# Two moves of VectorE and GpSimd work around the second and third output projections of a three-layer kernel

## The chip, the cores and the metric

The kernel runs on one core of one Trainium2 chip. The metric is the device time of one execution in microseconds (us). Before the change it was 1709.45 us, the median of three runs (1708.28 to 1711.23).

The core's engines each follow their own instruction list: TensorE (PE, matrix products), VectorE (DVE), ScalarE (ACT), GpSimd (POOL) and SyncE (SP), which here does nothing but issue loads and stores. They meet only at semaphores. An instruction whose semaphore has not been reached holds up everything behind it in the list of its engine, and on SP that means every later load.

## The reference, cut to what matters

One sequence of 256 tokens of width 1024 passes three layers. The first is a hybrid attention with a mixture of 16384 small experts. The other two are the same in form:

```python
mod = silu(c) @ ada_w[i] + ada_b[i]           # six vectors of 1024: shifts, scales, gates
h = modulate(rms_norm(x, g0), sh1, sc1)
y = mixer(h)                                  # i = 0: nsa; i = 1: sliding window ("swa"); each ends with o @ w_out
x = x + (1 + g1) * rms_norm(y, g1n)
h = modulate(rms_norm(x, g2n), sh2, sc2)
y = relu(h @ w_up)**2 @ w_down                # 1024 -> 4096 -> 1024
x = x + (1 + g2) * rms_norm(y, g3n)
```

The product `silu(c) @ ada_w` has one row, so it is not made by TensorE: VectorE multiplies a block of the transposed weights (128 output columns as partitions, 1024 inputs) by the broadcast row and sums. One such block is a "modulation block" or "piece" here. The last four vectors that are computed take 32 of them.

## The kernel before, in words

**Weights.** All weights except the modulation's come as a stream of 512 KB chunks (128 x 1024 floats) into a ring of eight slots. Chunk `c` may be loaded into its slot once chunk `c - 8` has been used (`chunk_used`). A product is made in three passes of reduced-precision parts: the high part of a chunk is rounded off by ACT (`high`, into one of four buffers, after chunk `c - 4` has been used), the low part is the difference of chunk and high part and is written over the chunk, by DVE or by POOL (`low`). A list, `BY_DVE`, says which chunks' low parts are DVE's; the rest of the split chunks are POOL's. TensorE waits for the low part of a chunk before it uses it. The first two chunks of some products are "pairs", whose high parts have buffers of their own (`pair_high`, `pair_low`).

**Stages.** The code of each engine is written out in the order of the stages. The ones that matter are: attention of the second layer (`att2`), its output projection (`out2`, eight chunks), end of the branch (`branch_end(0)`: y's squares by ACT, gating, residual sum and norm by DVE, transposes by TensorE, the high and low parts of the new activations), the MLP (`mlp2`, 64 chunks), `branch_end(1)`, the third layer's input projection with rotary embedding (`swa`, 10 chunks), attention (`att3`), output projection (`out3`, eight chunks), `branch_end(2)` and `mlp3`.

**The MLP.** Chunks of `w_up` and `w_down` alternate: in `mlp2`, up block `j` is chunk `2j - 2` for `j` from 2 to 29, and down block `j - 2` is chunk `2j - 1`; up 30 and 31 are chunks 58 and 59, and the last four down blocks are chunks 60 to 63. DVE's part is `hidden(name)`. Step `j` (0 to 31) squares ACT's relu of block `j` and splits it (`one(j)`), makes the low parts of one chunk (steps 0, 1, 30, 31) or of two, chunks `2j + 2` and `2j + 3` (steps 2 to 29), and, in `mlp2` only, uses one modulation piece (`ada(j)`): piece `j + 4`, in steps 0 to 27. Pieces 0 to 3 are used before that, in front of `branch_end(0)`.

**SP's order.** Modulation pieces have two buffers. `load_ada_mlp(i)` waits until piece `i - 2` has been used (`ada_used`), issues the load, and only then does SP come to the next chunk of the ring. In the MLP its loop is, for `k` from 0: load chunk `8 + 2k`, load piece `k + 6`, load chunk `9 + 2k`. Ahead of the loop SP issues pieces 0 and 1, chunks 0 to 3, pieces 2 and 3, chunks 4 to 7, pieces 4 and 5.

**Output projections.** In `out2` the low parts of the first four chunks are DVE's (two of them in the last two steps of `att2`, two after it) and POOL makes the other four. In `out3` all eight are POOL's.

Of the kernel before, what the change touches and what calls it, by code (L numbers as in the profile page):

```python
# [40 lines left out]
DB = D // P  # L41
# [10 lines left out]
HIGHS = 4  # L52
# [20 lines left out]
for _name, _n in STREAM:  # L73
# [12 lines left out]

BY_DVE = [FIRST_CHUNK[name] + i for name, first, n in [("qk1", 0, 2), ("wq", 2, 16), ("v", HIGHS, NKEYS), ("nsa", 2, 20), ("out2", 0, HIGHS),
                                                    ("mlp2", 2, 64), ("swa", 2, 10), ("mlp3", 2, 64)] for i in range(first, n)]
BY_POOL = [c for c in SPLIT if c not in BY_DVE]  # L90
NTH_BY_DVE = {c: i for i, c in enumerate(BY_DVE)}
NTH_BY_POOL = {c: i for i, c in enumerate(BY_POOL)}
# [140 lines left out]
ADA_LAYER3 = [A_NF + D, A_NF + 2 * D]  # L233
ADA_ORDER = [*range(6), 12, 13, 8, 9, 10, 6, 7, 11, 15, 16, 14, 17]
AT = {v: i for i, v in enumerate(ADA_ORDER)}
# [9 lines left out]
def two_blocks(nc, a):  # L245
    ctx = ExitStack()
    with ctx:
# [176 lines left out]
        def plan(kinds, unit0, step0, order=lambda s: 0):  # L424
            steps, unit = [], unit0
            for g in range(4):
                for t in range(TT):
                    ks = kinds(g)
                    for n, kind in enumerate(ks):
                        steps.append(dict(kind=kind, unit=unit, t=t, g=g, first=n == 0, last=n == len(ks) - 1))  # L430
                    unit += 1
            steps.sort(key=order)
            return [dict(s, n=step0 + i) for i, s in enumerate(steps)]
        att1 = plan(lambda g: ["moba" if g < 2 else "dsa"], 0, 0)
        att2 = plan(lambda g: ["sel", "win", "cmp"], 8, 8, lambda s: (s["g"], s["g"] == 0 and s["last"]))
        att3 = plan(lambda g: ["swa"], 16, 32)
# [5 lines left out]
        chunk = FIRST_CHUNK  # L442
# [186 lines left out]
        @block.gpsimd  # L629
        def _(pool):  # L630
            def low(c, more=0):
                pool.wait_ge(S["high_ready"], more + (NTH_SPLIT[c] + 1))
                pool.tensor_tensor(WL[:, c % SLOTS, :], ring[:, c % SLOTS, :], WH[:, c % HIGHS, :], ALU.subtract)\  # L633
                    .then_inc(S["low_by_pool"], 1)

            def lows(lo, hi):
                rounds = (hi - lo) // SLOTS
                if rounds:
                    with pool.Fori(0, rounds) as r:
                        for s in range(SLOTS):  # L640
                            low(lo + s, r * SLOTS)
                for c in range(lo + rounds * SLOTS, hi):
                    low(c)

            def split_done(n):
                pool.wait_ge(S["ht_low"], DB * (n + 1))
            pool.wait_ge(S["low_by_dve"], 2)
            lows(2, chunk["wq"])
            split_done(1)
            lows(chunk["u"], chunk["v"])  # L650
            lows(chunk["v"], chunk["v"] + HIGHS)
            pool.wait_ge(S["chunk_used"], chunk["nsa"] + 8)
            pool.memset(A(A_VCC, D + 4 * 2 * N_CMP), 0.0).then_inc(S["cmp_zeroed"], 1)  # L653
            lows(chunk["out2"] + HIGHS, chunk["mlp2"])
            lows(chunk["out3"], chunk["mlp3"])

        @block.tensor
# [995 lines left out]
        def _(dve):  # L1654
# [20 lines left out]
            def ada_piece(i, landed, slots, v, landed_more=0):  # L1675

                dve.wait_ge(S[f"{landed}{i % 2}"], landed_more + 16 * (i // 2 + 1))
                ada_block(A(slots[i % 2], D), v, i % DB)
# [34 lines left out]
            def low(c, more=0):  # L1713
                dve.wait_ge(S["high_ready"], more + (NTH_SPLIT[c] + 1))
                dve.tensor_tensor(WL[:, c % SLOTS, :], ring[:, c % SLOTS, :], WH[:, c % HIGHS, :], ALU.subtract)\  # L1715
                    .then_inc(S["low_by_dve"], 1)
# [81 lines left out]
            def attention(steps, beside=lambda i: None):  # L1798

                maxima(steps[0])  # L1800
                for i, s in enumerate(steps):
                    if i > 2 and steps[i - 3]["last"]:
                        y_low(steps[i - 3])
                    if i + 1 < len(steps):
                        maxima(steps[i + 1])
                    scale_probs(s)
                    beside(i)
                for s in steps[-3:]:
                    if s["last"]:
                        y_low(s)  # L1810
# [356 lines left out]
            for kv in range(2):  # L2167
                dve.wait_ge(S[f"z_loaded{kv}"], 64)
                for half_window in range(2):
                    first = 16 * half_window  # L2170
# [44 lines left out]
                    low(first + i)  # L2215

            def ada_mlp(i, r=None):
                ada_piece(i, "ada_mlp", ADA_LAYER3, 15 if i < DB and r is None else bass.ds(AT[15] + i // DB, 1) if r is None else
                          bass.ds(r + (AT[15] + i // DB), 1), 0 if r is None else r * (16 * DB // 2))

            def hidden(name):
                c0, o0, base = chunk["mlp" + name], OUTS["up" + name], 32 * (int(name) - 2)

                def ada(j, r=None):
                    if name == "2":
                        ada_mlp(j + 4, r)

                def one(j, more=0):
                    s = j % 2
                    dve.wait_ge(S["out_taken"], more + (o0 + j + 1))  # L2230
                    done = more + (base + j + 1)
                    dve.tensor_tensor(RELU[:, s, :], RELU[:, s, :], RELU[:, s, :], ALU.mult).then_inc(S["relu_squared"], 1)
                    dve.wait_ge(S["relu_squared"], done)
                    dve.tensor_copy(HIDH[:, j % HIDS, :], RELU[:, s, :]).then_inc(S["hidden_high"], 1)
                    dve.wait_ge(S["hidden_high"], done)
                    dve.tensor_tensor(HIDL[:, j % HIDS, :], RELU[:, s, :], HIDH[:, j % HIDS, :], ALU.subtract)\
                        .then_inc(S["hidden_ready"], 1)

                for j in range(2):
                    one(j)  # L2240
                    low(c0 + j + 4)
                    ada(j)
                for j in range(2, 4):
                    one(j)
                    low(c0 + 2 * j + 2)
                    low(c0 + 2 * j + 3)
                    ada(j)
                with dve.Fori(0, 3) as r:
                    for j in range(4, 12):
                        one(j, r * 8)  # L2250
                        low(c0 + 2 * j + 2, r * 16)
                        low(c0 + 2 * j + 3, r * 16)
                        ada(j, r)
                for j in (28, 29):
                    one(j)
                    low(c0 + 2 * j + 2)
                    low(c0 + 2 * j + 3)
                for j in (30, 31):
                    one(j)
                    low(c0 + 32 + j)  # L2260
# [1 line left out]
            low(chunk["out2"] + 2)  # L2262
            low(chunk["out2"] + 3)
            for i in range(2):
                ada_mlp(i)
            for i in range(2, 4):
                ada_mlp(i)
            for i in range(2):
                pair_low(chunk["mlp2"] + i)
# [12 lines left out]
                    low(chunk["swa"] + m + 2)  # L2282
                roped(ROPES3, ROPE2, lambda i: KD[:, i, :] if i < 2 else Q2[:, i - 2, :], m)
            dve.wait_ge(S["sink_loaded"], 16)
            attention(att3)
            for i in range(2):
                pair_low(chunk["mlp3"] + i)
            branch_end(2, chunk["mlp3"])
# [71 lines left out]
```

## Time and profile before

| what | value |
|---|---|
| median of three runs | 1709.45 us |
| the profiled execution, device time | 1708.28 us |
| its span in the profile | 1706.5 us |
| PE busy | 1638.2 us, 96% |
| VectorE busy | 1222.7 us, 72% |
| ScalarE busy | 908.9 us, 53% |
| GpSimd busy | 449.7 us, 26% |
| read from memory | 341 MB, 200 GB/s over the span |
| mean granted TensorE clock | 0.986 of full |

The span is the time from the first to the last instruction in the trace; 1.8 us lie around it. A busy share is a mean over stages that have different limits, so the question at each place is which wait ends last there.

### The profile page before, as it was taken

Reading aid. Unit: us, or ns where it says so; the run is one execution under the profiler, and the core shown is the slowest. Engines: PE = TensorE matmul, PEld = TensorE weight load, DVE = VectorE, ACT = ScalarE, POOL = GpSimd, SP = SyncE. Lnnn points to the kernel's source line nnn. Section 1 sums busy time; section 2 is a strip of 40 time slices with the busy share of each in tenths; the row PEclk is TensorE's granted clock in tenths of the full one; section 3 lists DMA queues with packets and bytes.
Section 4 is the critical chain, followed back from the end, with each engine's and each line's share of the span. In section 5 each row is a group of like instructions: output and inputs, shape, how many; then the busy total and the mean of one; then the engine's idle time right before and its main releaser. Section 6 shows DMA issues by size and latency. Waiting matters only on the chain.

```text
span 1706.5 us, 31170 instructions
## 1 busy us (share of the span) xinstructions
PE 1638.2 (96%) x10735; PEld 1442.5 (85%) x10740; DVE 1222.7 (72%) x2382; ACT 908.9 (53%) x1747; POOL 449.7 (26%) x181
## 2 busy tenths in 40 slices
PE   6988999999999998999999999998899999799998
PEld 3975899999999998788888878965699998489997
DVE  5369869599618993888877867747598877766665
ACT  4445554455469994454554565358544445664443
POOL 0970138989875556000000000000200000120000
PEclk9999999999999999999999999989999999999999
DMA  9877775555553334988888765540477766145553
GB/s 341 308 189 237 268 221 185 181 180 181 184 172 112 111 111 155 319 293 294 287 288 286 239 227 155 163 160 1 148 274 281 285 218 147 52 148 185 186 189 105
DMA packets 105527, 344.26 MB, mean 202 GB/s; under 512 B 18483, under 2 KB 22339, under 8 KB 105444
## 3 DMA queue, kind: packets, MB, share of 16 engines
q1 hardware_dynamic: 101092, 339.19, 59.3%
q10 hardware_dynamic: 4352, 4.02, 0.8%
q8 instruction: 46, 0.75, 0.2%
q14 instruction: 37, 0.30, 0.1%
HBM read 341.02 MB, written 1.10 MB: 200 GB/s over the span
## 4 chain that ended last, share of the span: by engine, by line
PE 80%; issue 5%; POOL 5%; DVE 4%; ACT 3%; DMA 2%; ACTq 1%; SPq 0%; POOLq 0%; DVEq 0%
PE banks L675 23%; PE banks L676 23%; PE banks L677 23%; POOL weights_low L633 5%; PE banks L981 3%; DMA ada_ring<-in_ada 1%; PE banks L840 1%; PE banks L807 1%; PE banks L856 1%; DMA arena<-in_ada 1%; ACT arena L1298 1%; PE banks L708 1%; PE banks L712 1%; PE banks L709 1%; DVE arena L1788 0%
## 5 line engine op out<-in xcount | busy, mean ns | idle before, releaser
L1244 ACT ACTIVATE weights_high<-ring 128x1024 fp32r<-128x1024 f32 x470 | 494.9, 1053 | 333.5 <-PE banks L677 321.4
L633 POOL TENSOR_TENSOR weights_low<-ring,weights_high 128x1024 fp32r<-128x1024 f32 x176 | 448.4, 2562 | 666.5 <-ACT weights_high L1244 666.0
L675 PE MATMUL banks<-ht_high,weights_high 128*128 128x256 f32 x1936 | 556.8, 288 | 4.1 <-DVE ht_low L1743 4.1
L676 PE MATMUL banks<-ht_low,weights_high 128*128 128x256 f32 x1936 | 547.9, 283 | 0.0
L677 PE MATMUL banks<-ht_high,weights_low 128*128 128x256 f32 x1936 | 547.8, 283 | 0.0
L1715 DVE TENSOR_TENSOR weights_low<-ring,weights_high 128x1024 fp32r<-128x1024 f32 x294 | 358.3, 1223 | 87.7 <-ACT weights_high L1244 86.9
L675 PEld LDWEIGHTS banks<-ht_high,weights_high 128*128 128x128 f32 x1936 | 371.2, 192 | 7.4 <-issue 4.1
L676 PEld LDWEIGHTS banks<-ht_low,weights_high 128*128 128x128 f32 x1936 | 371.5, 192 | 2.6
L677 PEld LDWEIGHTS banks<-ht_high,weights_low 128*128 128x128 f32 x1936 | 371.1, 192 | 0.0
L675 PE MATMUL banks<-weights_high,ga_parts 128*128 128x512 f32 x504 | 197.5, 392 | 9.3 <-DVE ga_parts L2047 9.2
L676 PE MATMUL banks<-weights_low,ga_parts 128*128 128x512 f32 x504 | 196.7, 390 | 0.0
L677 PE MATMUL banks<-weights_high,ga_parts 128*128 128x512 f32 x504 | 196.6, 390 | 0.0
L1500 ACT ACTIVATE ga_parts<-arena 128x256 fp32r (+1 forms) x126 | 52.5, 417 | 173.4 <-PE banks L677 173.4
L1666 DVE SCALAR_TENSOR_TENSOR arena<-arena,cs 128x1024 f32<-128x1024 f32 x80 | 106.5, 1342 | 50.0 <-DMA arena<-in_ada 45.0
L675 PEld LDWEIGHTS banks<-weights_high,ga_parts 128*128 128x128 f32 x504 | 95.0, 188 | 31.2 <-POOL weights_low L633 4.4
L677 PEld LDWEIGHTS banks<-weights_high,ga_parts 128*128 128x128 f32 x504 | 95.0, 189 | 19.9
L676 PEld LDWEIGHTS banks<-weights_low,ga_parts 128*128 128x128 f32 x504 | 95.1, 189 | 19.6
L653 POOL MEMSET arena<- 128x1144 f32 x1 | 1.1, 1052 | 390.3 <-PE banks L677 390.3
L675 PE MATMUL banks<-weights_high,hidden_high 128*128 128x512 f32 x256 | 100.3, 392 | 0.0
L676 PE MATMUL banks<-weights_low,hidden_high 128*128 128x512 f32 x256 | 100.3, 392 | 0.0
L677 PE MATMUL banks<-weights_high,hidden_low 128*128 128x512 f32 x256 | 99.6, 389 | 0.0
L2004 DVE TENSOR_TENSOR arena<-arena,banks 128x512 f32<-128x512 f32 (+1 forms) x64 | 44.0, 688 | 61.1 <-PE banks L981 55.6
(274 smaller groups left out, 2288.6 us busy)
## 6 DMA issues: line engine op xcount, KB each, us to landing
ring<-in_stream SPq DMA_DIRECT2D x490, 512.0 KB, 3.5
arena<-in_ada SPq DMA_DIRECT2D x88, 512.0 KB, 5.3
ada_ring<-in_ada SPq DMA_DIRECT2D x56, 512.0 KB, 4.3
arena<-gate_store SPq DMA_DIRECT2D x5, 512.0 KB, 5.9
arena<-bias_rows ACTq DMA_DIRECT2D x1, 2048.0 KB, 20.3
X<-in_x SPq DMA_DIRECT2D x1, 1024.0 KB, 6.1
out<-X SPq DMA_DIRECT2D x4, 256.0 KB, 2.1
arena<-arena ACTq DMA_DIRECT2D x8, 127.5 KB, 4.7
```

The costliest lines, as they stand in the source:

```text
L633: pool.tensor_tensor(WL[:, c % SLOTS, :], ring[:, c % SLOTS, :], WH[:, c % HIGHS, :], ALU.subtract)\
L675: pe.matmul(out, wh, xh, start=start, stop=False, **kw)
L676: pe.matmul(out, wh, xl, start=False, stop=False, **kw)
L677: return pe.matmul(out, wl, xh, start=False, stop=stop, **kw)
L708: pe.matmul(outs[n], wh[:, k * P:(k + 1) * P], HTH[:, k, :], start=i == 0 and n == 0, stop=False, skip_group_check=True)
L709: pe.matmul(outs[n], wl[:, k * P:(k + 1) * P], HTH[:, k, :], start=False, stop=False, skip_group_check=True)
L981: m = pe.matmul(banks[:, 2 + s, q * P:(q + 1) * P], onehot[:, s, 0, q, :], onehot[:, s, 1, q, :], start=True, stop=True)
L1244: act.activation(WH[:, c % HIGHS, :], ring[:, c % SLOTS, :], ACT.Copy).then_inc(S["high_ready"], 1)
L1500: act.activation(gated(j)[:, 0, :], src, ACT.Copy).then_inc(S["ga_high_ready"], 1)
L1666: dve.scalar_tensor_tensor(out=w, in0=w, scalar=1.0, in1=cs[:], op0=ALU.mult, op1=ALU.mult, accum_out=column)\
L1715: dve.tensor_tensor(WL[:, c % SLOTS, :], ring[:, c % SLOTS, :], WH[:, c % HIGHS, :], ALU.subtract)\
L2004: dve.tensor_tensor(g, g, banks[:, 2 + group % ONEHOTS, :].rearrange("p (t j) -> p j t", t=4), ALU.mult)\
```

## The change

The two pieces 2 and 3 are no longer used before `branch_end(0)`. `ada(j)` now uses piece `j + 2`, so that all pieces from 2 on lie two steps later in `hidden("2")`, and steps 28 and 29 get one each. SP's code is not touched. In `out3` the low parts of the first four chunks go from POOL to DVE: two in the last two steps of `att3`, two behind it.

```diff
 BY_DVE = [... ("nsa", 2, 20), ("out2", 0, HIGHS),
-                                                    ("mlp2", 2, 64), ("swa", 2, 10), ("mlp3", 2, 64)] for i in range(first, n)]
+                                                    ("mlp2", 2, 64), ("swa", 2, 10), ("out3", 0, HIGHS), ("mlp3", 2, 64)] for i in range(first, n)]
...
             lows(chunk["out2"] + HIGHS, chunk["mlp2"])
-            lows(chunk["out3"], chunk["mlp3"])
+            lows(chunk["out3"] + HIGHS, chunk["mlp3"])
...
                 def ada(j, r=None):
                     if name == "2":
-                        ada_mlp(j + 4, r)
+                        ada_mlp(j + 2, r)
...
                 for j in (28, 29):
                     one(j)
                     low(c0 + 2 * j + 2)
                     low(c0 + 2 * j + 3)
+                    ada(j)
...
             for i in range(2):
-                ada_mlp(i)
-            for i in range(2, 4):
                 ada_mlp(i)
...
-            attention(att3)
+
+            def beside_att3(step):
+                if step >= len(att3) - 2:
+                    low(chunk["out3"] + step - (len(att3) - 2))
+            attention(att3, beside_att3)
+            for i in range(2, HIGHS):
+                low(chunk["out3"] + i)
```

VectorE's list at the end of `out2`. L1666 is a modulation piece, L1720 the low part of a pair, L2196 the gating of y; `ada_mlp0` and `ada_mlp1` are the landings in the two buffers:

```order
 L1666 SCALAR_TENSOR_TENSOR arena,mod<-arena,cs 128x1024 [waits ada_mlp0]
 L1666 SCALAR_TENSOR_TENSOR arena,mod<-arena,cs 128x1024 [waits ada_mlp1]
-L1666 SCALAR_TENSOR_TENSOR arena,mod<-arena,cs 128x1024 [waits ada_mlp0]
-L1666 SCALAR_TENSOR_TENSOR arena,mod<-arena,cs 128x1024 [waits ada_mlp1]
 L1720 TENSOR_TENSOR weights_low<-ring,pair_high 128x1024 [waits pair_high] x2
 L2196 TENSOR_TENSOR arena<-banks,arena 128x512 [waits y_sums,gate_rows_ready]
```

Two pieces, and the wait for their landing, have left the place between `out2` and the gating of its result.

SyncE's list at the start of `mlp2`, which is the same before and after (L477 loads a modulation piece, L469 a chunk of the ring):

```order
L477 DMA arena<-in_ada 128x1024 [waits ada_used] x2
L604 UNCONDITIONAL_BRANCH
L604 ISA
L469 ISA [waits chunk_used]
L469 DMA ring<-in_stream 128x1024
L474 ISA
L477 ISA [waits ada_used]
L477 DMA arena<-in_ada 128x1024
L467 REGISTER_ALU
L469 ISA [waits chunk_used]
L469 DMA ring<-in_stream 128x1024
```

Nothing moved here: each load of a piece still stands ahead of a load of a chunk, and waits for a piece that VectorE now uses two steps later.

VectorE's list at the end of `att3`. L1788 scales probabilities, L1795 is a low part of the attention's result, L1715 the low part of a chunk:

```order
 L1788 TENSOR_SCALAR arena<-arena,rsum 128x256 [waits dve_link]
 L1788 TENSOR_SCALAR arena<-arena,rsum 128x256 x3
+L1715 TENSOR_TENSOR weights_low<-ring,weights_high 128x1024 [waits high_ready]
 L1795 TENSOR_TENSOR ht_low<-banks,ht_high 128x2x128 [waits y_high_ready] x3
+L1715 TENSOR_TENSOR weights_low<-ring,weights_high 128x1024 [waits high_ready] x2
 L1720 TENSOR_TENSOR weights_low<-ring,pair_high 128x1024 [waits pair_high] x2
```

Three of the four low parts are seen here, and the fourth stands one attention step earlier; in GpSimd's list four of the eight for `out3` are gone.

## Rows read from the trace of the kernel before

**Rows 1.** The page: the span, and the chain that ended last.

```profile
span 1706.5 us, 31170 instructions
...
PE 80%; issue 5%; POOL 5%; DVE 4%; ACT 3%; DMA 2%; ACTq 1%; SPq 0%; POOLq 0%; DVEq 0%
```

**Rows 2.** Timeline, VectorE, end of out2: start, duration, operation, idle time before and releaser.

```profile
1216.08 1.23 DVE L1666 SCALAR_TENSOR_TENSOR arena<-arena,cs 128x1024 f32<-128x1024 f32 x1 [11.83 <-DMA arena<-in_ada]
...
1218.52 2.36 DVE L1720 TENSOR_TENSOR weights_low<-ring,pair_high 128x1024 fp32r<-128x1024 f32 x2
...
1232.65 0.54 DVE L1730 TENSOR_SCALAR ht<-banks,scl,mod 128x256 f32<-128x256 f32 x1 [2.18 <-PE banks L736]
```

**Rows 3.** Timeline, ScalarE: first square of y, out2 and out3.

```profile
1215.98 0.60 ACT L1228 ACTIVATE arena<-banks 128x512 f32<-128x512 f32 x1 [1.23 <-PE banks L677]
...
1507.78 0.60 ACT L1228 ACTIVATE arena<-banks 128x512 f32<-128x512 f32 x1 [1.69 <-PE banks L677]
```

**Rows 4.** Timeline, VectorE: first activation block after out3.

```profile
1519.81 0.54 DVE L1730 TENSOR_SCALAR ht<-banks,scl,mod 128x256 f32<-128x256 f32 x1 [0.60 <-PE banks L736]
```

**Rows 5.** Timeline, SyncE, steady loop of mlp2: start, time to the last issue's end.

```profile
1301.65 3.21 SPq L469 DMA_DIRECT2D ring<-in_stream  x2
1305.15 0.33 SPq L477 DMA_DIRECT2D arena<-in_ada  x1
1307.27 3.21 SPq L469 DMA_DIRECT2D ring<-in_stream  x2
```

**Rows 6.** Timeline, VectorE, steady loop of mlp2.

```profile
1302.61 1.23 DVE L1715 TENSOR_TENSOR weights_low<-ring,weights_high 128x1024 fp32r<-128x1024 f32 x1 [0.99 <-ACT weights_high L1244]
1303.75 1.22 DVE L1666 SCALAR_TENSOR_TENSOR arena<-arena,cs 128x1024 f32<-128x1024 f32 x1
...
1306.02 1.22 DVE L1715 TENSOR_TENSOR weights_low<-ring,weights_high 128x1024 fp32r<-128x1024 f32 x1
```

**Rows 7.** Timeline, ScalarE, steady loop of mlp2: high part of a down chunk.

```profile
1301.51 1.06 ACT L1244 ACTIVATE weights_high<-ring 128x1024 fp32r<-128x1024 f32 x1 [1.33 <-PE banks L677]
```

**Rows 8.** Timeline, SyncE, start of mlp2's loop.

```profile
1243.88 0.34 SPq L477 DMA_DIRECT2D arena<-in_ada  x1
1244.48 1.37 SPq L469 DMA_DIRECT2D ring<-in_stream  x2
```

**Rows 9.** DMA issues, 1244.4 to 1244.6 us: count, size, us to landing.

```profile
ring<-in_stream SPq DMA_DIRECT2D x1, 512.0 KB, 4.8
```

**Rows 10.** One source line, L469, 1243 to 1380 us: all its loads.

```profile
DMA to landing us min/median/max: 3.4/4.0/6.5
```

**Rows 11.** Windows: busy us by engine (PE, PEld, DVE, ACT, POOL), PE clock, DMA share, GB/s.

```profile
1306.00:1328.00 22.00, 22.00 (x143) 20.12 (x142) 17.80 (x28) 9.30 (x12) 0.00 (x0) 1.00 0.78 284
```

**Rows 12.** Timeline, VectorE: piece of step 2, and the low part of chunk 59.

```profile
1250.42 1.22 DVE L1666 SCALAR_TENSOR_TENSOR arena<-arena,cs 128x1024 f32<-128x1024 f32 x1
...
1392.53 1.23 DVE L1715 TENSOR_TENSOR weights_low<-ring,weights_high 128x1024 fp32r<-128x1024 f32 x1 [0.99 <-ACT weights_high L1244]
```

**Rows 13.** Timeline, ScalarE: first square of y after mlp2.

```profile
1407.59 0.60 ACT L1228 ACTIVATE arena<-banks 128x512 f32<-128x512 f32 x1 [1.56 <-PE banks L677]
```

**Rows 14.** Timeline, GpSimd: low parts of out3's first three chunks.

```profile
1446.63 7.72 POOL L633 TENSOR_TENSOR weights_low<-ring,weights_high 128x1024 fp32r<-128x1024 f32 x3 [231.88 <-ACT weights_high L1244]
```

**Rows 15.** One source line, L2136 (rotary product from the arena): ns min/median/max.

```profile
L2136 DVE TENSOR_TENSOR arena<-arena,onehot x18: 424/425/2428, 1050.3 to 1458.8; 128x256 f32<-128x256 f32 x18
```

**Rows 16.** Timeline, TensorE: last rotation, second score group of att3, start of out3.

```profile
1455.50 0.70 PE L1046 MATMUL banks<-arena 128*128 128x256 f32 x2 [0.98 <-ACT arena L1639]
...
1460.18 2.08 PE L807 MATMUL banks<-arena 64*128 64x256 f32 x8 [3.01 <-DVE arena L2138]
...
1491.35 0.50 PE L675 MATMUL banks<-weights_high,ht_high 128*128 128x512 f32 x1
```

**Rows 17.** Windows, start of att3.

```profile
1460.00:1470.00 10.00, 8.51 (x46) 4.75 (x46) 7.35 (x25) 5.72 (x28) 0.00 (x0) 0.77 0.07 28
```

**Rows 18.** Timeline, VectorE, last step of att3.

```profile
1486.52 0.16 DVE L1778 TENSOR_TENSOR sums<-sums,dsink 128x4 f32<-128x4 f32 x1 [1.49 <-ACT dsink L1302]
```

More of the change, by code:

```diff
@@ L2217, in ada_mlp @@
             def ada_mlp(i, r=None):
-                ada_piece(i, "ada_mlp", ADA_LAYER3, 15 if i < DB and r is None else bass.ds(AT[15] + i // DB, 1) if r is None else
-                          bass.ds(r + (AT[15] + i // DB), 1), 0 if r is None else r * (16 * DB // 2))
+                first = AT[15] + i // DB
+                ada_piece(i, "ada_mlp", ADA_LAYER3, bass.ds(first, 1) if r is None else bass.ds(r + first, 1),
+                          0 if r is None else r * (16 * DB // 2))
             def hidden(name):
```

## The prediction

> **What bounds the kernel now.** I read the page first: TensorE carries 80% of the chain that ended last [rows 1], so a change counts only where TensorE waits, or where it makes TensorE wait. Then I read the engines' timelines at the three places that the edit touches: the end of out2, the loop of mlp2, and the stretch from the end of swa to the start of out3.
>
> At the end of out2 ScalarE begins to square y at 1215.98 [rows 3], but VectorE is then at modulation pieces 2 and 3, whose data it got only at 1216.08 after 11.83 us without work, and at the pair's low parts from 1218.52 [rows 2]. The gating of y comes behind them, and the first block of new activations at 1232.65, 16.67 us after the square. Out3 has the same sequence without pieces in front: 1507.78 to 1519.81, 12.03 us [rows 3, 4].
>
> In mlp2 TensorE is busy without a gap (22.00 of 22 us at full clock [rows 11]). A step of the loop takes 5.62 us: SP's issues at 1301.65 and 1307.27 [rows 5]. What the reader is to see in rows 5 and 6 is who lets SP go on. VectorE starts its piece at 1303.75 and is through with it at 1304.97; SP issues the next piece at 1305.15, at once. So SP stands already now at the wait for `ada_used`, and what holds it is the piece of VectorE's current step. After it comes the load of chunk 9 + 2k at 1307.27, which waits for its ring slot.
>
> At the end of swa GpSimd makes its low parts from 1446.63 on, three in 7.72 us and the fourth behind them [rows 14]. In this stretch VectorE's rotary products, 0.425 us otherwise, take up to 2.428 [rows 15], and TensorE then stands for 3.01 us until 1460.18 [rows 16].
>
> **Part 1, pieces 2 and 3 leave the end of out2.** Without them the pair's low parts can be made as soon as ScalarE has the high parts, as in out3, and the gating waits for the square only. I take the difference of the two sequences: 16.67 - 12.03 = 4.6 us gained. Bounds: nothing, or 1218.52 - 1216.08 + 2.36 = 4.8, all that now stands between.
>
> **Part 2, every piece is used two steps later.** VectorE's own work in the loop stays the same. The queue behind it does not. SP's load of piece k + 6 waits for piece k + 4. That was used in step k; it is now used in step k + 2. Queued behind this wait on SP is the load of chunk 9 + 2k, whose low part VectorE makes in step k + 3, the very next one. The lead of three steps becomes one.
>
> Does the ring's reserve cover it? Take the chunk that is issued at 1307.27. Piece k + 4 is now used two steps after 1304.97, at 1316.21. SP issues the piece at 1316.39 and the chunk 0.60 us later (1243.88 to 1244.48 [rows 8]), at 1316.99. The low part of this chunk is begun now at 1302.61 + 3 x 5.62 = 1319.47, and its high part at 1301.51 + 3 x 5.62 = 1318.37 [rows 6, 7]. So 1.4 us are left between issue and high part. A chunk issued 0.60 us behind a piece took 4.8 us to land [rows 9]. It is 3.4 us late.
>
> And the delay feeds itself, since the piece of step k + 3 stands behind this low part, and frees the load of the next down chunk. The circle from one step's piece to the next one's is:
> - VectorE's piece starts, to SP's issue of the next piece: 1303.75 to 1305.15, 1.40
> - to the issue of the chunk: 0.60
> - landing: 4.8
> - ScalarE's high part starts, to the low part's start: 1301.51 to 1302.61, 1.10
> - low part's start to the next piece's start: 1302.61 to 1303.75, 1.14
>
> Together 9.04 us, against 5.62 us that TensorE needs for the two chunks. TensorE starves as soon as its own reserve is used up.
>
> How many times? The first down chunk behind such a wait is 9 (k = 0, low part in step 3), the last 59 (k = 25, low part in step 28, behind piece 31, the last one). That is 26 circles. The piece of step 2 starts at 1250.42 [rows 12]; it would start there still, if the steps before it were not shifted by part 1. The piece of step 28 then starts at 1250.42 + 26 x 9.04 = 1485.5, where the low part of chunk 59 is finished now at 1393.7 (1392.53 + 1.14 [rows 12]). Behind it VectorE has the piece and `one(29)`, 2.27 (1303.75 to 1306.02 [rows 6]), two low parts, 2.28, piece and `one(30)`, 2.27, a low part, 1.14, `one(31)`, 1.13, and the low part of chunk 63, 1.14: 10.2 us, to 1495.7. TensorE then has half a chunk for the first half of y, 5.62 / 4 = 1.4. The first square starts at 1497.1 instead of 1407.59 [rows 13]: 89.5 us later. The two pieces that steps 28 and 29 get are in this sum.
>
> The uncertain term is the landing. The trace shows 3.4 us at best and 6.5 at worst for loads of this line in this stretch [rows 10]; the loop now moves three transfers in 5.62 us with the DMA engines 0.78 busy [rows 11], and in 9 us the queue would be emptier, so the upper end is unlikely. 26 circles make this 36.4 us less, or 44.2 us more. I take 4.8, since it was measured on the same sequence, piece and then chunk. With 3.4 us for a load alone [rows 10] and three transfers in 0.78 of 5.62 us [rows 11], so 1.46 each, the estimate by that rule is 3.4 + 1.46 - 0.60 = 4.3 us, and 13 us less in the sum; the row's 4.8 is longer, and the sum goes by the row.
>
> **Part 3, out3's first four low parts by VectorE.** GpSimd no longer works beside the rotary products. The last rotation's result is there at 1456.2 (1455.50 + 0.70 [rows 16]), the last unit of three short VectorE operations takes 3 x 0.425 [rows 15], so TensorE can go on at about 1457.6 instead of 1460.18: 2.6 us. With the stand of 3.01 us gone, the granted clock need not fall. It is 0.77 over the ten us behind it [rows 17], and eight matmuls and the mask behind them take 2.08 us and more at the lower level, about 1.3 us of which comes back. Together 4.0 us gained; bounds 0 (if it were not the POOL work) and 5.
>
> Its cost: VectorE waits 1.49 us in the last step of att3 [rows 18], longer than the 1.14 of a low part put in front of it. The second one lies where VectorE waits for ScalarE to take the last values; the third and fourth are needed 2 and 3 chunks after TensorE starts out3 at 1491.35 [rows 16], and VectorE has nothing else then. I cost them at nothing; if the cover is gone they cost at most two low parts, 2.3 us.
>
> **The sum**, against the profiled execution: 1706.5 - 4.6 + 89.5 - 4.0 = 1787.4 us of span, and 1.8 us around it: 1789.2. That execution was the fastest of the three, 1.2 us below the median. I predict 1789.
>
> **Rivals.**
> - *The ring covers the wait.* If a chunk landed in less than the 1.4 us left, or if SP's wait were for an older piece than I read, nothing of part 2 would appear, and the change would be faster: 1708.3 - 4.6 - 4.0 = 1699.7. For it: SP's wait costs nothing now, although it already ends with VectorE's piece, and VectorE idles 0.99 us per step [rows 6]. Against it: the fastest landing is 3.4 us [rows 10], and the count of steps is fixed by the code. It decides in favour of faster if the chunk can be issued 3.4 us earlier than 1316.99. 6%.
> - *The circle is there, but short.* With landings of 3.4 us it is 7.64 us, and the time is 1789 - 36 = 1753. This is the lower end of my forecast's own case.
> - *TensorE's clock falls in the gaps.* It would stand for almost 3 us per circle, and after the stand of 3.01 us at 1460.18 the clock was low [rows 16, 17]. If it stayed at half, two chunks would take 11.24 us, more than the circle, and set the step: 26 x 2.2 = 57 us more, 1846. Against it: at half clock TensorE would have no gaps, and nothing would keep it there. 4%.
> - *Part 3 does nothing or costs*: 1789 + 4 + 2 = 1795, inside the range.
>
> **How the numbers follow.** Forecast with its own spread of landings 88%, covered wait 6%, low clock 4%, something not foreseen that leaves the time near that of before 2%. The range of 1755 to 1825 holds landings from 3.5 to 6.2 us and the doubt on part 3, and leaves out the covered wait, the low clock and the extremes. A measurement of this kernel tells a change of about 0.2% from none. Faster by more: 0.06; within: 0.02; slower: 0.92.
>
> **What would show it.** In the profile after, the waits of mlp2: ScalarE's high part (L1244) should wait for the DMA into the ring, once per step, and TensorE for VectorE's low part. SP's issues of pieces should be about 9 us apart instead of 5.62, with the chunk 0.6 us behind each. The window of mlp2 should last some 90 us longer with TensorE at 60 to 65% and the DMA share near 0.5. From the first square of y to the first block after out2 there should be 12 us. The rotary products should all take 0.42 us, and TensorE's stand before the second score group should be gone. If the issues of pieces stay 5.6 us apart, part 2 is wrong, and with it the forecast.

## The result and the profile after

The change makes the kernel slower: 1781.59 us (median of 4 runs, 1780.21 to 1783.8) against 1710.12 us (median of 4, 1708.28 to 1711.23), a ratio of 1.0417 [1.0404, 1.043]. The forecast was 1789, with a range of 1755 to 1825. The profiled execution took 1781.99 us, with a span of 1780.0 us at a mean granted clock of 0.976, against 1706.5 us of span before [rows 1]. Ratios here and below are of fast runs alone: one run of the kernel before, in the batch of piece_first, short_pieces and busy_gap, took 3902.38 us and is left out.

The page of the kernel after, the span and the chain that ended last:

```profile
span 1780.0 us, 31167 instructions
...
PE 68%; DMA 8%; issue 7%; DVE 6%; ACT 5%; POOL 5%; SPq 1%; ACTq 1%; POOLq 0%; DVEq 0%
```

TensorE's share of the chain falls from 80% [rows 1] to 68%, and DMA's rises from 2% to 8%: the kernel now waits for weights in a place where it did not.

The timelines give the two spans in stages that meet end to end (us; the squares are ScalarE's L1228, the block is VectorE's L1730):

| stage | before | after | difference |
|---|---|---|---|
| start to first square of y in out2 | 1215.98 | 1216.80 | +0.8 |
| to the first activation block | 16.67 | 12.03 | -4.6 |
| mlp2, to its first square of y | 174.94 | 256.26 | +81.3 |
| swa, to att3's second score group (TensorE, L807) | 52.59 | 50.02 | -2.6 |
| att3, to TensorE's start of out3 | 31.17 | 29.78 | -1.4 |
| to the end | 215.15 | 215.11 | 0.0 |

All of the loss lies in mlp2. The waits of the engines in that stretch (1230 to 1490 us) in the kernel after: who waited for whom, us in total, times, longest:

```profile
ACT weights_high L1244 <- DMA ring<-in_stream: 167.7, 38, 7.2
DVE weights_low L1715 <- ACT weights_high L1244: 106.7, 27, 5.4
PE banks L675 <- DVE weights_low L1715: 51.8, 42, 3.0
```

and those of SyncE's queue:

```profile
SPq L477 <- DVE arena L1666: 197.0, 28, 16.6
SPq L469 <- PE banks L677: 18.2, 6, 9.7
```

Read from the bottom up this is the whole story. SyncE stood 197 us in front of the loads of pieces (L477), for a piece that VectorE had not yet used. Before, from 1225 to 1410 us, its waits were:

```profile
SPq L469 <- PE banks L677: 112.4, 54, 6.5
...
SPq L477 <- DVE arena L1666: 10.7, 7, 3.6
```

It stood for TensorE in front of the chunks (L469), which is where a ring that is full should hold it. The chunks behind the waiting load came late, so ScalarE waited for DMA, VectorE for ScalarE, and TensorE for VectorE.

One round of the circle, in the kernel after. Timeline of SyncE's queue (start, us, idle time before and releaser in brackets):

```profile
1337.94 0.33 SPq L477 DMA_DIRECT2D arena<-in_ada  x1
1338.53 0.92 SPq L469 DMA_DIRECT2D ring<-in_stream  x2
1346.35 0.33 SPq L477 DMA_DIRECT2D arena<-in_ada  x1
```

ScalarE:

```profile
1342.71 1.06 ACT L1244 ACTIVATE weights_high<-ring 128x1024 fp32r<-128x1024 f32 x1 [6.13 <-DMA ring<-in_stream]
```

VectorE:

```profile
1336.54 1.22 DVE L1666 SCALAR_TENSOR_TENSOR arena<-arena,cs 128x1024 f32<-128x1024 f32 x1
...
1343.81 1.23 DVE L1715 TENSOR_TENSOR weights_low<-ring,weights_high 128x1024 fp32r<-128x1024 f32 x1 [3.77 <-ACT weights_high L1244]
1344.95 1.22 DVE L1666 SCALAR_TENSOR_TENSOR arena<-arena,cs 128x1024 f32<-128x1024 f32 x1
```

The piece starts at 1336.54 and SP issues the next one 1.40 us later, the chunk 0.59 behind it. ScalarE takes the chunk up 4.18 us after that (1338.53 to 1342.71), the low part starts 1.10 later, and the next piece 1.14 later: 8.41 us, five terms in the order of the forecast. Beside 5.62 us before [rows 5] this round is 2.8 us too long. Over the whole loop, from the piece of step 2 (1246.59) to that of step 28 (1473.75), 26 rounds took 227.16 us, 8.74 us each. Of the 25 intervals between SP's issues of pieces, 20 lie between 8.4 and 8.8 us and five between 9.1 and 10.0. The five long ones are rounds in which the chunk itself landed late: from its issue to ScalarE's high part it took 4.9 to 5.8 us there, 4.2 to 4.6 in the other 21 rounds, and 4.55 in the mean.

TensorE in the same round, and windows over the loop (busy us of PE, PEld, DVE, ACT, POOL, then the granted clock, DMA share, GB/s):

```profile
1336.76 0.69 PE L675 MATMUL banks<-weights_high,hidden_high 128*128 128x512 f32 x1 [2.60 <-DVE weights_low L1715]
...
1339.80 0.63 PE L676 MATMUL banks<-weights_low,hidden_high 128*128 128x512 f32 x1
1340.23 0.43 PE L677 MATMUL banks<-weights_high,hidden_low 128*128 128x512 f32 x1
```

```profile
1262.00:1460.00 198.00, 152.94 (x811) 128.36 (x809) 104.62 (x161) 53.57 (x69) 0.00 (x0) 0.91 0.50 179
1306.00:1328.00 22.00, 15.13 (x78) 12.57 (x77) 11.74 (x18) 6.94 (x9) 0.00 (x0) 0.89 0.44 152
```

The second window is that of [rows 11], where TensorE was busy for all 22 us at a DMA share of 0.78. In the round shown TensorE stands for 2.60 us, works some 3.5 us at 1.2 GHz (0.63 us a matmul), and then at 2.4 GHz (0.43 and 0.40). Such a slow stretch comes in 12 of the 26 rounds, about every second one.

The end of out2 in the kernel after, ScalarE and VectorE, to set beside [rows 2, 3]:

```profile
1216.80 0.60 ACT L1228 ACTIVATE arena<-banks 128x512 f32<-128x512 f32 x1 [2.15 <-PE banks L677]
```

```profile
1204.39 3.41 DVE L1666 SCALAR_TENSOR_TENSOR arena<-arena,cs 128x1024 f32<-128x1024 f32 x1
...
1210.44 6.38 DVE L1720 TENSOR_TENSOR weights_low<-ring,pair_high 128x1024 fp32r<-128x1024 f32 x2 [2.63 <-ACT pair_high L1248]
1217.58 1.52 DVE L2196 TENSOR_TENSOR arena<-banks,arena 128x512 f32<-128x512 f32 x2 [0.76 <-ACT arena L1228]
...
1228.83 0.54 DVE L1730 TENSOR_SCALAR ht<-banks,scl,mod 128x256 f32<-128x256 f32 x1 [0.61 <-PE banks L736]
```

The pair's low parts are now made ahead of the square, and the gating (L2196) waits for the square alone. They take 6.38 us instead of 2.36 [rows 2], since GpSimd still makes its own low parts there, but they end at 1216.82, before the gating could start: a cost on VectorE that nobody waits for.

The end of swa, the one line of the rotary products (ns min/median/max), and TensorE:

```profile
L2136 DVE TENSOR_TENSOR arena<-arena,onehot x18: 424/425/426, 1051.4 to 1533.7; 128x256 f32<-128x256 f32 x18
```

```profile
1533.00 0.70 PE L1046 MATMUL banks<-arena 128*128 128x256 f32 x2 [0.98 <-ACT arena L1639]
...
1535.11 1.13 PE L807 MATMUL banks<-arena 64*128 64x256 f32 x8 [0.43 <-DVE arena L2138]
...
1564.89 0.50 PE L675 MATMUL banks<-weights_high,ht_high 128*128 128x512 f32 x1
```

The longest rotary product fell from 2.428 us [rows 15] to 0.426, TensorE's stand from 3.01 [rows 16] to 0.43. The eight matmuls behind it take 1.13 us instead of 2.08.

### The profile page after: what moved, and what is told of

The parts are those of the page before. It is cut to its first block, busy times and chain, and to the rows that moved or that the text cites. A ratio compares the mean times of both kernels' runs of the same rounds, so it can differ in the third digit from the quotient of the medians.

```text
span 1780.0 us, 31167 instructions
## 1 busy us (share of the span) xinstructions
PE 1665.9 (94%) x10735; PEld 1456.2 (82%) x10740; DVE 1227.1 (69%) x2386; ACT 906.6 (51%) x1747; POOL 439.6 (25%) x177
## 4 chain that ended last, share of the span: by engine, by line
PE 68%; DMA 8%; issue 7%; DVE 6%; ACT 5%; POOL 5%; SPq 1%; ACTq 1%; POOLq 0%; DVEq 0%
PE banks L675 19%; PE banks L676 19%; PE banks L677 19%; DMA ring<-in_stream 7%; POOL weights_low L633 5%; PE banks L981 3%; DVE arena L1666 2%; ACT weights_high L1244 2%; DMA ada_ring<-in_ada 1%; PE banks L840 1%; DVE weights_low L1715 1%; PE banks L856 1%; PE banks L807 1%; ACT arena L1298 1%; SPq L477 1%
## 5 line engine op out<-in xcount | busy, mean ns | idle before, releaser
L633 POOL TENSOR_TENSOR weights_low<-ring,weights_high 128x1024 fp32r<-128x1024 f32 x172 | 438.3, 2560 | 750.6 <-ACT weights_high L1244 750.2
L1715 DVE TENSOR_TENSOR weights_low<-ring,weights_high 128x1024 fp32r<-128x1024 f32 x298 | 363.3, 1223 | 170.4 <-ACT weights_high L1244 169.6
L675 PE MATMUL banks<-weights_high,hidden_high 128*128 128x512 f32 x256 | 110.0, 430 | 46.6 <-DVE weights_low L1715 46.6
L1666 DVE SCALAR_TENSOR_TENSOR arena<-arena,cs 128x1024 f32<-128x1024 f32 x80 | 110.1, 1387 | 34.7 <-DMA arena<-in_ada 29.4
L677 PE MATMUL banks<-weights_high,hidden_low 128*128 128x512 f32 x256 | 107.2, 419 | 0.0
L676 PE MATMUL banks<-weights_low,hidden_high 128*128 128x512 f32 x256 | 107.1, 418 | 0.0
L675 PEld LDWEIGHTS banks<-weights_high,hidden_high 128*128 128x128 f32 x256 | 52.2, 204 | 62.3 <-issue 48.4
```

Source lines behind the costliest of these rows:

```text
L675: pe.matmul(out, wh, xh, start=start, stop=False, **kw)
L676: pe.matmul(out, wh, xl, start=False, stop=False, **kw)
L677: return pe.matmul(out, wl, xh, start=False, stop=stop, **kw)
L1666: dve.scalar_tensor_tensor(out=w, in0=w, scalar=1.0, in1=cs[:], op0=ALU.mult, op1=ALU.mult, accum_out=column)\
```

## The experiments

Ratios are to the kernel before, run in the same batch on the same chip. Stages as in the table above: out2's end | mlp2 | swa to the second score group | from there to TensorE's start of out3 and on to its first square of y. The last one is 47.60 us before and 46.21 after.

### One part at a time

**p3_only**: the kernel before with part 3 alone.

```diff
-                                                    ("mlp2", 2, 64), ("swa", 2, 10), ("mlp3", 2, 64)] for i in range(first, n)]
+                                                    ("mlp2", 2, 64), ("swa", 2, 10), ("out3", 0, HIGHS), ("mlp3", 2, 64)] for i in range(first, n)]
...
-            lows(chunk["out3"], chunk["mlp3"])
+            lows(chunk["out3"] + HIGHS, chunk["mlp3"])
...
-            attention(att3)
+
+            def beside_att3(step):
+                if step >= len(att3) - 2:
+                    low(chunk["out3"] + step - (len(att3) - 2))
+            attention(att3, beside_att3)
+            for i in range(2, HIGHS):
+                low(chunk["out3"] + i)
```

> The kernel before with only the second half of the change: VectorE makes the low parts of out3's first four chunks. Theory (GpSimd's low parts stretched VectorE's rotary products, and TensorE's stand lowered its clock): 4.0 us less than before, 1706 us; 2.6 of it ahead of the second score group of att3, 1.3 behind it. Rival A (only the stretching counts): 2.6 us less. Rival B (no effect, or VectorE pays for it in att3): 0 to 2 us more.

Measured: 1706.74 us (10 runs), ratio 0.9977 [0.9967, 0.9988]. Stages 14.99 | 174.94 | 50.02 | 49.05. Its rotary products and TensorE's timeline:

```profile
L2136 DVE TENSOR_TENSOR arena<-arena,onehot x18: 424/425/427, 1052.5 to 1455.7; 128x256 f32<-128x256 f32 x18
```

```profile
1457.06 2.00 PE L807 MATMUL banks<-arena 64*128 64x256 f32 x8 [0.43 <-DVE arena L2138]
```

and the granted clock (last but two of the columns) in two windows:

```profile
1457.00:1462.00 5.00, 4.22 (x20) 2.31 (x20) 2.64 (x8) 2.08 (x12) 0.00 (x0) 0.66 0.54 171
1462.00:1470.00 8.00, 6.92 (x40) 3.63 (x42) 6.08 (x23) 5.19 (x22) 0.00 (x0) 0.79 0.00 0
```

So the 2.6 us of the stretching is confirmed to 0.03 us (52.59 - 50.02 = 2.57). The 1.3 us of the clock is not: the stand is down to 0.43 us, and the clock falls all the same, so that this execution gives 1.45 us back (49.05 - 47.60). The medians of the batch cannot decide between the two sizes: the interval of the ratio stands for 2.1 to 5.6 us, and holds 4.0 as well as 2.6.

**pieces_only**: the full change without part 3. Against the full change:

```diff
-                                                    ("mlp2", 2, 64), ("swa", 2, 10), ("out3", 0, HIGHS), ("mlp3", 2, 64)] for i in range(first, n)]
+                                                    ("mlp2", 2, 64), ("swa", 2, 10), ("mlp3", 2, 64)] for i in range(first, n)]
...
-            lows(chunk["out3"] + HIGHS, chunk["mlp3"])
+            lows(chunk["out3"], chunk["mlp3"])
...
-            attention(att3, beside_att3)
-            for i in range(2, HIGHS):
-                low(chunk["out3"] + i)
+            attention(att3)
```

> The kernel before with only the first half: pieces 2 and 3 leave the place before the branch end, all others two steps later. Theory (the circle of piece, load, landing, high part, low part): the whole loss is here, 1710 - 4.6 + 81.3 = 1786 us. Rival (part of the loss comes from out3's low parts on VectorE, or from both halves together): clearly less than 1786.

Measured: 1787.58 us, ratio 1.0449 [1.0428, 1.0469]. Stages 12.01 | 255.94 | 53.10 | 48.94. The stages add up: mlp2 is as long as in the full change, out2's end as short, and swa's end as in before. Part 3 beside it is worth 53.10 - 50.02 + 48.94 - 46.21 = 5.8 us in the profiled executions, of which 2.7 lie in the stage that the clock moves; the medians, of two batches, differ by 6.0.

### The loss in mlp2: what the chunks are queued behind

**chunk_ahead**: the full change, and SyncE issues both chunks of a step ahead of the step's piece. The waits themselves are as they were.

```diff
                     load_chunk(beside + 2 * k, r * (2 * DB))
-                    load_ada_mlp(k + 6, r * DB)
                     load_chunk(beside + 2 * k + 1, r * (2 * DB))
+                    load_ada_mlp(k + 6, r * DB)
```

(the same in the eight steps behind the loop)

> The changed kernel with two lines of SP's loop swapped: both chunks of an iteration are issued ahead of the piece. VectorE's order and the waits stay. Theory: the chunks behind a piece's wait are now needed two steps later instead of one. The circle over two steps is 1.40 to the piece, 0.6 and 0.35 to the second chunk, 4.3 to 5.7 to land, 1.10, 1.14, so 8.9 to 10.3 us against 11.24 of two steps: hidden, 1710 - 8.6 = 1701.5 us. Rival A (the piece's own wait or its landing is what costs, not what stands behind it): still about 1780. Rival B (the DMA engines cannot serve the bunched loads): between, 1720 to 1760.

Measured: 1701.28 us, ratio 0.9944 [0.9925, 0.9963]. Stages 12.03 | 174.93 | 50.01 | 46.21. SyncE's queue still stands before the pieces, 1225 to 1410 us:

```profile
SPq L477 <- DVE arena L1666: 115.3, 28, 16.6
SPq L469 <- PE banks L677: 18.5, 8, 6.5
```

and TensorE has no gap:

```profile
1306.00:1328.00 22.00, 22.00 (x143) 20.04 (x142) 19.77 (x30) 10.76 (x13) 0.00 (x0) 1.00 0.86 305
```

This is what tells the order in the queue from everything else. The pieces are used as late as in the full change, VectorE does the same work, as many bytes move, and SyncE waits in 28 of its piece loads, as in the full change. Only what stands behind that wait differs: the next step's chunks now, whose low parts are due two steps on instead of one. A circle of about 9 us now spans two steps, 11.24 us of TensorE's work, and 81 us are gone.

**loads_later**: the full change, and SyncE loads piece k + 4 in step k (pieces 0 to 3 ahead of the loop), so that its wait is for the piece used in that same step again.

```diff
-            for k in (0, 2, 4):
+            for k in (0, 2):
...
-                if k < 4:
-                    load_chunks(ahead + 2 * k, ahead + 2 * k + 4)
+                load_chunks(ahead + 2 * k, ahead + 2 * k + 4)
...
-                    load_ada_mlp(k + 6, r * DB)
+                    load_ada_mlp(k + 4, r * DB)
```

(the same in the steps behind the loop)

> The changed kernel with SP's piece loads moved back by two iterations, as VectorE's uses were: iteration k loads piece k + 4, and only pieces 0 to 3 are loaded ahead. Theory: SP's wait ends again in the step in which it ended before the change, so mlp2 takes what it took, and both gains stay: 4.6 + 4.0, 1701.5 us, less up to 0.5 for the pieces of steps 28 and 29. Rival (moving pieces into steps 28 and 29 or the loads' new places cost something of their own): 1703 to 1710.

Measured: 1701.8 us, ratio 0.9946 [0.9931, 0.9961]. Stages 12.02 | 174.93 | 50.02 | 47.79. SyncE's waits are nearly those of the kernel before again (in this kernel the lines have numbers smaller by one):

```profile
SPq L469 <- PE banks L676: 113.0, 56, 6.5
...
SPq L477 <- DVE arena L1665: 11.5, 9, 3.6
```

**piece_first**: the full change, SyncE untouched; in each step of mlp2 VectorE uses the piece right behind `one(j)`, ahead of the step's low parts.

```diff
                     for j in range(4, 12):
                         one(j, r * 8)
+                        ada(j, r)
                         low(c0 + 2 * j + 2, r * 16)
                         low(c0 + 2 * j + 3, r * 16)
-                        ada(j, r)
```

(the same in the steps before and behind this loop)

> The changed kernel with SP untouched; in each step of mlp2 VectorE uses the piece ahead of the low parts instead of behind them. Theory: the low part that waits for the late chunk then no longer stands ahead of its own step's piece, so the circle runs over two steps: 1.40 + 0.6 + 4.3 (landing) + 1.10 + 1.14 to the end of the low part + 1.13 for the next step's hidden block = 9.7 us against 11.24: hidden, 1701.5 us. Rival (what counts is how many steps late the pieces are used, not the order inside the step): 1780, as the changed kernel.

Measured: 1703.54 us, ratio 0.9963 [0.9949, 0.9976]. Stages 12.03 | 174.95 | 50.02 | 47.67. SyncE waits for the pieces in 28 loads, 113.1 us together, and mlp2 does not become longer by it. The chunk behind the wait for the piece of step k + 2 still has its low part in step k + 3, but the piece of step k + 3 now stands ahead of that low part, and only the piece of step k + 4 behind it. The circle again spans two steps, 11.24 us. Two edits on different engines thus do the same to it. The stages tell this version from loads_later by 0.1 us; the medians differ by 1.7, with overlapping intervals.

### The size of the circle: what the landing is made of

**short_pieces**: the full change, with pieces 6 to 31 loaded with 128 of their 1024 columns. VectorE still works over all 1024, over old values for the rest, so that its times stay and only the bytes ahead of the chunk go.

```diff
-                load_ada(k, ADA_LAYER3, ADA_BEFORE["mlp2"] + k - 1, 14 * DB + k, "ada_mlp", more)
+                if k < 6 and isinstance(more, int):
+                    load_ada(k, ADA_LAYER3, ADA_BEFORE["mlp2"] + k - 1, 14 * DB + k, "ada_mlp", more)
+                    return
+                sp.wait_ge(S["ada_used"], more + (ADA_BEFORE["mlp2"] + k - 1))
...
+                sp.dma_start(A(ADA_LAYER3[k % 2], 128), src[:, 0:128]).then_inc(S[f"ada_mlp{k % 2}"], 16)
```

> The changed kernel, but pieces 6 to 31 are loaded with 128 of their 1024 columns (the rest of the buffer keeps older values, so the last modulation vectors are wrong in value). Theory: the down chunk lands late because its piece's bytes are ahead of it in the queues; without them it lands in 3.5 us, the circle is 7.7 instead of 8.74, and the time is 1782 - 26 x 1.0 = 1756 us. Rival (the landing of the chunk is its own, or the chunk behind slows it): about 1780.

Measured: 1760.16 us, ratio 1.029 [1.0274, 1.0306]. Stages 12.02 | 233.62 | 50.03 | 49.05. mlp2 took 233.62 us instead of 256.26, so 22.64 / 26 = 0.87 us less per round. DMA issues of one chunk behind a piece, to landing, in the full change (1338.4 to 1338.7 us):

```profile
ring<-in_stream SPq DMA_DIRECT2D x1, 512.0 KB, 4.1
```

and in this kernel (1335.7 to 1336.0 us):

```profile
ring<-in_stream SPq DMA_DIRECT2D x1, 512.0 KB, 3.6
```

Taking seven eighths of the transfer ahead away brings the chunk down near to the 3.4 us of a load alone [rows 10]. A rival by which the landing is a latency that has nothing to do with the piece ahead gives nothing here, and falls. The chunk behind is still issued as close as before, and the landing is within some 0.2 us of a load alone, so it is not what delays the chunk. The 0.87 us is a mean of two things: the even rounds became some 0.7 us shorter, and the long landings of 4.9 to 5.8 us are gone (the longest is now 4.15 us to the high part). Why some landings were that long in the full change stays open; that shorter pieces end them is all that this run shows.

### The clock at the start of att3

**busy_gap**: the kernel before, with 13 matmuls without use (`keep_busy(13, 6)`) in the gap of 3.01 us.

```diff
+                    if s["n"] == att3[0]["n"]:
+                        keep_busy(13, 6)
```

> The kernel before, with 13 idle-time matmuls (2.8 us at full clock) put on TensorE between the first and the second score group of att3, in the gap of 3.01 us. GpSimd's low parts and the stretched rotary products stay. Theory (the gap lowered the clock): the second score group takes 1.13 us instead of 2.08, TensorE's part behind it likewise, and the kernel is 1.0 to 1.4 us faster, 1708.8 against 1710.1. Rival (the clock has another cause): the group still takes about 2 us, no gain.

Measured: 1711.76 us (11 runs), ratio 1.0001 [0.9989, 1.0012]. Stages 17.57 | 174.93 | 55.91 | 47.80. TensorE:

```profile
1459.72 4.52 PE L754 MATMUL banks<-const,ident_b 128*128 128x512 bf16 x13
1464.17 1.14 PE L807 MATMUL banks<-arena 64*128 64x256 f32 x8
...
1468.76 0.65 PE L840 MATMUL banks<-const,arena 128*128 128x128 f32 x4 [1.94 <-DVE arena L1790]
1469.42 1.86 PE L807 MATMUL banks<-arena 64*128 64x256 f32 x8
```

The second group now runs at full clock (1.14 us instead of 2.08), but the clock fell in the fill itself (0.52 over 1460 to 1463 us) and again later, at 1469.42 (0.85 over 1470 to 1480 us). From the second group to out3's first square it is 47.80 us, against 47.60 before. The run is not a clean test. In this execution a stretched rotary product lay ahead of the first score group, and VectorE was through with the last one at 1461.21 us, so that the gap would have been at most 1.5 us; the fill took 4.52 and held the second group back until 1464.17 us, which is most of the 3.3 us by which the stage grew (52.59 to 55.91). It shows that a stretch at the lower clock also comes without that stand, and nothing on what a fill of the right length would gain. That the stand does not decide rests on p3_only, where it is down to 0.43 us and the stretch is there.

## Why the prediction was right

The sign and the mechanism came out as forecast, and the sum was 7.4 us of span too high (1787.4 against 1780.0). By its steps:

**Part 1**, -4.6 forecast, -4.64 measured (16.67 to 12.03). The size is right, but one of its causes was missed. In p3_only the pieces still stand in front, TensorE stands as long before the norm's transposes (3.56 us, 3.66 in before), and the stage takes 14.99 us: there the clock stays at full, while in before it is 0.50 over 1226 to 1229 us. The transposes in before and in p3_only:

```profile
1225.72 1.97 PE L736 MATMUL banks<-const,arena 128*128 128x128 f32 x8 [3.66 <-DVE arena L1704]
```

```profile
1226.75 1.09 PE L736 MATMUL banks<-const,arena 128*128 128x128 f32 x8 [3.56 <-DVE arena L1704]
```

At full clock the pieces cost 14.99 - 12.03 = 2.96 us; the other 1.68 us are a lower clock that the profiled execution of before had and another had not. I had read 16.67 - 12.03 as the price of the pieces' time alone, and that the sum came out to 0.04 us is partly luck: with the pieces in front the stage took 14.99, 16.67 and, in busy_gap, 17.57 us, without them 12.01 to 12.03 in all six executions. TensorE's stand is 3.56 to 3.66 us with them and 0.52 to 0.54 without, so the lower clock may itself come of the pieces; no run takes the two apart.

**Part 2, the mechanism**: all five arcs of the circle, the terms of its sum, are there in their order, one round per step, 26 of them, and chunk_ahead and piece_first, which let it span two steps, and loads_later, which lets SP go on two steps earlier, each get the whole 81 us back. One reading on the way was wrong. I had SP stand at the wait for the piece in the steady loop of before already. Its waits there are for TensorE, in front of the chunks: from 1262 to 1385 us 85.4 us in 44 waits, and 0.5 us in two for a piece. In [rows 5, 6] SP is through with the chunk's issue at 1304.86 and the piece ends at 1304.97: SP comes to that wait as it ends. The count of steps, on which the forecast hangs, is the code's and did not need that reading. **Its size**: forecast 9.04 us a round, measured 8.74 in the mean and 8.4 to 8.8 in most. The four other arcs came out as read (1.40, 0.53 to 0.60, 1.10, 1.14 in most rounds); the landing was mis-sized. I took 4.8 from one load at the loop's start [rows 9]; in the 26 rounds it is 4.55 in the mean and 4.18 in the round shown, counted to the start of the high part some 0.1 us behind the landing. The two rounds at the loop's start took 5.2, so a row from there was not typical of the loop. The 0.30 us a round, most of it the landing and the rest the chunk's closer issue, are 26 x 0.30 = 7.8 us, the whole miss but for a tail that was 0.3 shorter (11.34 from the last piece to the square, 11.6 forecast) and a square in out2 that came 0.8 later. The estimate by the ring order in the Trainium skill ("DMA: Bandwidth & Descriptors", Queues, rings and completion order) had given 4.3, with the chunk delayed by the piece ahead of it and not by the chunk behind. It was the nearer one: the 21 rounds without a long landing lie at 4.2 to 4.6, 4.39 in the mean, and short_pieces bears out that it is the piece ahead that delays. The estimate had 1.46 - 0.60 = 0.86 us for this delay; the even rounds show some 0.7, and the 0.87 of the mean holds the long landings too, so that its closeness is chance.

**Part 3**, -4.0 forecast, -2.57 - 1.39 = -3.96 measured in the full change; alone it gives a ratio of 0.9977, which is 3.9 us, with an interval of 2.1 to 5.6. The 2.6 us of stretching are shown. The 1.3 us of clock have the right size in this profiled execution and in chunk_ahead's (46.21 both), but the reason I gave fell: p3_only has a stand of only 0.43 us and the low clock all the same. From the second group to the square it took 47.6 to 49.1 us in the executions with a lower clock (before, p3_only, pieces_only, loads_later, piece_first, short_pieces, busy_gap), 46.21 in the two without. Of the six profiled executions with part 3 in them four had the lower clock, so it is luck that the full change's execution shows the 1.39 us. What sets the clock there stays open. The cover held: in att3's last two steps VectorE made both low parts (1558.00 and 1561.53) and ScalarE's values were taken without delay, TensorE starting out3 29.78 us after the second group, 31.17 before.

**The rivals.** "The ring covers the wait" fell: in 28 loads SyncE waited, and the issues lay 8.74 us apart. "Part 3 does nothing" fell with p3_only. "TensorE's clock falls in the gaps" was half right: it does fall, in the loop the mean is 0.91, but only for some 3.5 us in about every second round, and since a round is set by the circle, in which TensorE has no part, this costs nothing. It did spoil one of my signs. I had looked for a TensorE at 60 to 65%, and it shows 152.94 of 198 us, 77%. Two chunks in 8.74 us would be 64%. A mean clock of 0.91 stands for 0.18 x 198 = 36 us at half clock, work that takes 18 us at full clock, so 18 of the 26 us too many; the rest may lie in the modelled ends of the matmuls. The signs that do not hang on the clock came out: a wait of ScalarE's high part for DMA in every step (in some a second one), the chunk 0.59 behind the piece, the DMA share at 0.50, 12.03 us in out2, rotary products at 0.42.

## What to carry to other kernels

A queue that issues loads in order holds back every load behind the one that waits, so when work is moved, count for each load not only when its own buffer comes free but which unrelated load stands behind it, and how many steps later that one is due; here a lead that fell from three steps to one cost 81 us in one stage, and swapping two lines of issue order (chunks first, 1701.28 us, ratio 0.9944 [0.9925, 0.9963]) made the same change faster than the kernel before. A circle that feeds itself is sized by adding its arcs once and multiplying by the rounds, and its least known arc, read from one load, deserves a second estimate from how the transfers overlap. And a stage's length that is read off one execution can hold a stretch of lower clock: compare it with a second execution before the whole is put down to the work that goes.

## What the runs showed of the hardware

- A load of 512 KB issued 0.53 to 0.60 us behind another one in most rounds is taken up 4.2 to 4.6 us after its issue in 21 of 26 rounds and 4.9 to 5.8 in five (mean 4.55). With seven eighths of the one ahead removed the mean is 3.68, and a round is 0.87 us shorter.
- VectorE's operations with two SBUF inputs stretch beside GpSimd's low parts: rotary products from 0.425 to 2.428 us, a piece from 1.22 to 3.41, a pair of low parts from 2.36 to 6.38. With GpSimd's work gone, all 18 products take 0.424 to 0.427. The Trainium skill ("SBUF — State Buffer", SBUF: two separate sides) calls it an exclusive lock on a shared port, in which the loser waits for the other's whole instruction; the traces agree as far as the excess of one operation (2.00 and 2.19 us) stays below GpSimd's 2.56 us for one low part.
- The granted clock fell to 1.2 GHz for some 3.5 us in 12 of the 26 rounds of the slow loop, and not in the others, though TensorE stood in every round from the second on. In short_pieces' loop it stood so too, 1.5 to 2.0 us in nearly every round, and the clock fell in one. The same matmul that follows a stand of 3.56 us in p3_only's out2 runs at full clock and the one behind 3.66 us in before's at half (1.09 and 1.97 us for the eight of L736), and at the start of att3 the clock fell behind a stand of 0.43 us in p3_only and in short_pieces, and not in the full change and chunk_ahead, where it is 0.43 too. How long TensorE stood does not tell by itself, in this kernel, whether the clock falls.
